# Hybrid decoder trunk: the low part of each weight block is subtracted by VectorE in place of GpSimd

## What is computed

```python
# layer 0: gated linear attention + retention; layer 1: mLSTM + RG-LRU (conv, gates, linear scan)
for each layer:
    h = rmsnorm(x, g_mix)
    p = h @ W_in                      # split into q, k, v, gates of the two mixers
    x = x + concat(mixer_a(p), mixer_b(p)) @ W_out
    h = rmsnorm(x, g_ffn)
    x = x + (silu(h @ W_gate) * (h @ W_up)) @ W_down
y = rmsnorm(x, g_final)
# outputs: y of prompt and samples, and the new states of every mixer
```

## Time and profile before

| | value |
|---|---|
| time, median of 3 runs (lowest, highest) | 2683.19 us (2681.18, 2689.47) |
| profiled execution, own time | 2684.99 us |
| its span | 2683.0 us |
| mean granted TensorE clock in it | 0.963 of full speed |
| PE busy | 2510.4 us, 94% |
| DVE busy | 1090.7 us, 41% |
| ACT busy | 894.8 us, 33% |
| POOL busy | 1263.5 us, 47% |
| `weights_lo` on POOL, 396 instructions | 950.5 us |

### The profile page before, as it was taken

How to read it: one execution, slowest core, us unless ns; L and a number is a source line. 1 busy time by engine, 2 the same in 40 slices (tenths; PEclk the granted TensorE clock), 3 DMA queues, 4 the chain that set the end, 5 groups by cost and what they waited for, 6 DMA issues and landing times.

```text
span 2683.0 us, 36878 instructions
## 1 busy us (share of the span) xinstructions
PE 2510.4 (94%) x15666; PEld 2248.5 (84%) x15666; DVE 1090.7 (41%) x1682; ACT 894.8 (33%) x1173; POOL 1263.5 (47%) x670
## 2 busy tenths in 40 slices
PE   7999998999999999899977899999877999999997
PEld 5889986888887888899967889978765879999997
DVE  3413343534426412534364641154575345222224
ACT  4332344332113413343243331344342133222222
POOL 5654455554445744343433464435423346455553
PEclk9999998999999999999988999999987999999999
DMA  4222241213123222222211122222212233222222
GB/s 156 94 79 70 72 155 64 71 71 122 63 79 110 89 99 98 70 73 79 97 53 63 63 97 95 90 69 79 92 63 80 71 102 119 86 89 85 95 95 79
DMA packets 72322, 233.17 MB, mean 87 GB/s; under 512 B 8768, under 2 KB 10848, under 8 KB 72160
## 3 DMA queue, kind: packets, MB, share of 16 engines
q1 hardware_dynamic: 72160, 230.82, 25.1%
HBM read 221.74 MB, written 9.05 MB: 86 GB/s over the span
## 4 chain that ended last, share of the span: by engine, by line
PE 75%; DVE 10%; POOL 4%; POOLq 3%; issue 3%; ACT 2%; DVEq 1%; DMA 1%; SPq 0%; ACTq 0%
PE ps L666 53%; PE ps L696 16%; POOLq L1171 3%; POOL wl L1165 2%; DVE xc L1665 1%; DVE xc L1686 1%; DVE mixl L1492 1%; DMA wr<-in_wblk 1%; DVE sq L1294 1%; ACT wh L954 1%; POOL sq L1246 1%; PE ps L755 0%; PE ps L753 0%; POOL rsA L1177 0%; PE ps L775 0%
## 5 line engine op out<-in xcount | busy, mean ns | idle before, releaser
L1165 POOL TENSOR_TENSOR wl<-wr,wh 128x1024 fp32r<-128x1024 f32 (+2 forms) x396 | 950.5, 2411 | 585.4 <-ACT wh L954 585.0
L666 PE MATMUL ps<-xh,wh 128*128 128x260 f32 (+3 forms) x3312 | 897.7, 325 | 18.7 <-DVE xl L1307 16.6
L666 PE MATMUL ps<-xh,wl 128*128 128x260 f32 (+3 forms) x3312 | 883.3, 321 | 0.0
L666 PE MATMUL ps<-xl,wh 128*128 128x260 f32 (+3 forms) x3312 | 882.2, 321 | 0.0
L666 PEld LDWEIGHTS ps<-xh,wh 128*128 128x128 f32 (+1 forms) x3312 | 551.1, 189 | 76.8 <-issue 24.2
L666 PEld LDWEIGHTS ps<-xh,wl 128*128 128x128 f32 (+1 forms) x3312 | 549.4, 188 | 48.4 <-issue 1.4
L666 PEld LDWEIGHTS ps<-xl,wh 128*128 128x128 f32 (+1 forms) x3312 | 549.9, 189 | 46.3 <-issue 1.7
L954 ACT ACTIVATE wh<-wr 128x1024 fp32r<-128x1024 f32 (+2 forms) x396 | 408.7, 1045 | 459.0 <-DMA wr<-in_wblk 454.5
L696 PE MATMUL ps<-hidh,wh 128*128 128x260 f32 (+1 forms) x1056 | 293.4, 332 | 54.8 <-DVE xB L1502 26.1
L1044 ACT ACTIVATE sq<-sq 128x512 f32<-128x512 f32 (+1 forms) x88 | 55.9, 635 | 699.6 <-DVE sq L1294 699.5
L696 PE MATMUL ps<-hidl,wh 128*128 128x260 f32 (+1 forms) x1056 | 288.8, 328 | 0.0
(11 more groups left out here) (329 smaller groups left out, 2357.8 us busy)
## 6 DMA issues: line engine op xcount, KB each, us to landing
wr<-in_wblk SPq DMA_DIRECT2D x392, 512.0 KB, 3.3
xr<-in_xT SPq DMA_DIRECT2D x8, 260.0 KB, 5.6
xB<-in_xT SPq DMA_DIRECT2D x8, 260.0 KB, 4.7
out_yT<-xB SPq DMA_DIRECT2D x8, 260.0 KB, 2.2
xr<-in_xT SPq DMA_DIRECT2D x8, 256.0 KB, 5.6
xA<-in_xT SPq DMA_DIRECT2D x8, 256.0 KB, 4.8
Ss<-in_s_even SPq DMA_DIRECT2D x1, 2048.0 KB, 11.2
out_ss_even<-Ss SPq DMA_DIRECT2D x1, 2048.0 KB, 9.5
```

Source lines behind the costliest of these rows:

```text
L666: mm = pe.matmul(ps[0:cols, b + c, 0:n], wt[:, w], xt[:, e:e + n], start=first, stop=end)
L1165: pool.tensor_tensor(wl[n % 4][:, 0:w], wr[n % 4][:, 0:w], wh[n % 4][:, 0:w].bitcast(F32), ALU.subtract).then_inc(s_lo, 1)
```

## The change

The subtraction `wl = wr - wh` is issued by DVE in place of POOL, at the same item of the common list, with the same operands, the same wait (`s_hi`, set by ACT) and the same increment (`s_lo`). SP, ACT and PE have the same instructions in the same order as before.

```diff
         @block.gpsimd
         def _(pool):
-            def weights_lo(n):
-                w = block_cols(n)
-                pool.wait_ge(s_hi, n + 1)
-                pool.tensor_tensor(wl[n % 4][:, 0:w], wr[n % 4][:, 0:w], wh[n % 4][:, 0:w].bitcast(F32),
-                                   ALU.subtract).then_inc(s_lo, 1)
...
             for k, *v in pl.items:
-                if k == "w":
-                    weights_lo(v[0])
-                elif k == "xs":
+                if k == "xs":
...
         @block.vector
         def _(v):
+            def weights_lo(n):
+                w = block_cols(n)
+                v.wait_ge(s_hi, n + 1)
+                v.tensor_tensor(wl[n % 4][:, 0:w], wr[n % 4][:, 0:w], wh[n % 4][:, 0:w].bitcast(F32),
+                                   ALU.subtract).then_inc(s_lo, 1)
...
             for it in pl.items:
                 k, *z = it
-                if k == "xs":
+                if k == "w":
+                    weights_lo(z[0])
+                elif k == "xs":
```

## The result

The changed kernel takes 2710.47 us in the median (2705.48 to 2714.41, 5 runs), against 2688.11 us (2681.18 to 2694.76, 5 runs) for the kernel before. The ratio is 1.0072, with a 95% interval from 1.0057 to 1.0087: slower by 0.7%, some 19 us (the medians differ by 22).

A forecast was written before the change was run, and what follows sets the result against it. PE was taken to bound the kernel (busy 94% of the span). Losses 41 + 7 + 15 = 63 us against gains of 36 gave net +27 us: 2712 on the profiled execution, 2710 us for the median, range 2668 to 2738.

The forecast's parts named there:

- The 18 places: Half B down units: subtraction delays d1's addition on DVE, PE stands 2.3 us at each, 41 us (bounds 32 and 63).
- Half A: Down units with four in flight: the subtraction stays hidden from PE, with 0.3 us to spare.
- The duration: One DVE subtraction of 1024 columns: taken as 1.25 us, bounds 0.75 and 2.43 us.
- POOL's side: Subtractions leave POOL's queue: gains at Q, `wl`, rsB and the start, 18.5 us in all, 7 of them for `wl`.
- the start: First 24 us, PE busy 7.61: one subtraction less on POOL's path gains 2.5 us.
- rsB: Sum of squares behind a POOL subtraction: of PE's 5.9 us of waits the longest, 3.0 us, goes.
- Q: POOL's attention operand: PE waits for it three times, 9.3 us, of which 6 us were to go.
- The release of DVE: DVE instructions with two SBUF inputs no longer stretched beside POOL's subtraction: 10 us gained, with 7 us of clock.
- its new load: DVE's subtractions in about eleven scan and gate-row places: 7 us lost, bounds -7 to +32.
- qnm: PE's wait of 7.5 us for DVE, behind two blocked instructions: 2 us gained, net of one added subtraction.
- The rival of a faster kernel: Stages with scans: DVE's release weighs more, 51 us plus POOL's 18.5, 70 us of gains, 2661 us; chance 0.16.
- The clock: Granted clock behind 18 new PE stalls: 15 us lost, bounds 0 and 29; 7 us gained from avoided idle times.

The follow-up runs named there:

- e1: Changed kernel, but on DVE the 18 subtractions behind the addition of down unit d0 in half B stand behind that of d2: 2666.97 us, 0.9916.
- e2: Changed kernel, but the same 18 subtractions are done by POOL with a semaphore of their own: 2666.19 us, 0.9914.
- e3: Kernel before, with only the 18 subtractions behind d0 of half B on DVE and the other 378 on POOL: 2742.91 us, 1.0191.
- e6: Kernel before, POOL still subtracts but PE neither reads nor waits for the low part, the third pass multiplying the high part: 2690.78 us, 1.0003.
- e5: No engine subtracts; the third pass multiplies the high part and PE waits for ACT's rounding alone: 2578.39 us, 0.9587 to the kernel before.
- e8: As e6, but POOL fills the slot with two memsets in place of the subtraction, reading nothing from SBUF: 2599.81 us, 0.9668.
- e4: Changed kernel, with a second DVE instruction of the same size and a drain ahead of each of the 18 subtractions: 2752.85 us, 1.0234.

## Why the prediction was right, and where it wasn't

**The 18 places** were put at 41 us of stalls and 15 of clock. The stalls measure 2.0 us in place of 2.3 (the subtraction takes 1.22 us and PE starts at once), the ten of the last feed-forward 20 us. With the clock the 18 cost 42 us by e1 and e2, 51 by e3. The mechanism and its place were right. Only 15 of the 18 places have a wait of their own, so the stalls are 31 us in place of 41. The clock fell behind 8 of the 15, which is 14 us: taking half was right here, though no row before spoke for half rather than for none or all.

**Half A** was held to be hidden, with 0.3 us to spare. Nearly: four waits for xA of 0.6 to 1.7 us show in the changed kernel that weren't in the timeline of before, 4.4 us in all.

**The duration** on DVE, 1.25 us: 1.22 alone, 1.31 in the mean.

**POOL's side**: the start gained (PE is busy 9.45 us of the first 24 against 7.61), rsB gained its 3.0 us, `wl` its 7.5 in the profile though e6 says that these were worth nothing. Q was to gain 6 us and gained 1.2. The forecast took one subtraction out of POOL's queue and left POOL's other instructions as long as they were; but now they meet the subtraction on DVE. Ahead of the longest of these waits the last instruction of Q takes:

```profile
442.27 2.11 DVE L1283 TENSOR_TENSOR wl<-wr,wh 128x1024 fp32r<-128x1024 f32 x1 [1.64 <-ACT wh L954]
...
443.26 1.43 POOL L1191 TENSOR_TENSOR Q<-qk,EQ 64x128 f32<-64x128 f32 x1
```

It took 0.46 us in the kernel before, and the first instruction of K ahead of it, beside another subtraction, 2.09 us in place of 1.26. So the stretching goes both ways: from the start of `sq` to the end of Q, POOL took 13.2 us in place of 13.5, though a subtraction of 2.4 us had gone from between them.

**The release of DVE and its new load** are the step that failed, twice and in opposite senses. I put the gains at 36 us in all, and DVE's load in the scans and gate rows at 7. By e5 and e6, POOL's subtraction cost 112 us; by e1 and e5, DVE's costs 88. The difference, 23 us in favour of DVE (e1 against before), is near the 29 that I had. I had added up the few waits of PE whose last releaser was visibly held, and even of `qnm` I took 2 us where e5 gives back 6.5 with three stretched instructions ahead of it. In a chain of DVE instructions every stretched one adds to one wait of PE, which the profile puts down to the last instruction alone. That is shown for `qnm`; for the other waits in the mixers and scans it is my reading. Lost clock comes on top (0.977 over the span in e5, 0.962 in e6). The same holds for the 1.3 us that DVE got: nearly all of the 88 us lie in the same three stretches. The rival of a faster kernel came nearer to the size of the release, with 70 us of the 112, and lacked that price.

So the sum holds two pairs of errors that cancel: release and load, 36 and 7 in place of 112 and 88, and within the losses 56 us for the 18 places in place of 42. The net of +19 was met within 8 us, but mechanism and size hold together only for the 18 places.

**The clock**: 0.963 before, 0.961 after. From 1750 to 2220 it rose from 0.92 to 0.93; from 1085 to 1530 it fell from 0.95 to 0.93 and in the last stage from 1.00 to 0.99.

## What to carry to other kernels

Moving an instruction to a faster engine also moves its wait: look at what stands behind it in the new queue and who holds a buffer for that, above all where fewer buffers are in flight. Here 18 of 396 instructions turned a gain of 0.8% into a loss of 0.7%, and two down units further down the list they took nothing from the last stage. To price a load on an engine in a latency-bound stretch, leave the work out once: the waits in a profile name only the last link of a chain.

## What the runs showed of the hardware

- A DVE instruction with two inputs in SBUF is stretched beside a POOL subtraction (8 columns: 2.40 us in place of 0.22) and not beside POOL's memsets (0.22 us in all 12 of e8). Two memsets in place of the subtraction gave back 90 us of 2689.
- Instructions with one input were stretched too: beside the subtraction a copy of 32 columns to 2.33 us from 0.18 and a TENSOR_SCALAR of 4x512 to 2.47 from 0.42 (e6 and e5), beside the memsets a TENSOR_SCALAR of 512 columns to 0.94 from 0.43 in the mean (e8 and e5).
- It goes both ways: a POOL product of 64x128 took 1.43 us beside a subtraction on DVE, and 0.46 before.
- A DVE subtraction of 128x1024 float32 takes 1.22 us and one of 128x512 0.69, where POOL takes 2.43 for 128x1024.
- Stalls of PE of about 2 us in a stream of matmuls brought the granted clock down behind 8 of 15; where it fell, the group of 34.6 us took 38.5 rather than 36.8. Stalls of 3.2 to 3.7 us did so behind 10 of 10 (e4).
